# Three joints of a three-block network kernel: the last square goes into the means by matmul, a table load is issued ahead, first matmuls wait for less, and branch outputs are rounded in two steps

## The reference, cut to what matters

```python
def rms_norm(x, g):
    xf = x.astype(jnp.float32)
    y = xf * lax.rsqrt(jnp.mean(xf * xf, axis=-1, keepdims=True) + EPS)
    return (y * g.astype(jnp.float32)).astype(x.dtype)
...
# first block, end of the mixer
y = gates[:, :, 0] * y_a + gates[:, :, 1] * y_b + gates[:, :, 2] * y_c
return y @ lp['w_out'], s_f, s_b
...
# first block
h_lat = h_lat + g1 * yl
h_lat = h_lat + g2 * swiglu(modulate(rms_norm(h_lat, norm2_g[l]), sh2, sc2), w_ffn_in[l], w_ffn_out[l])
...
# second block ends in a feed-forward layer and a norm; the third begins with a norm and a projection
return _rmsnorm(x, final_norm)
...
h = rms_norm_3(x, norm_g) * (1.0 + scale[:, None, :]) + shift[:, None, :]
z = h @ w_in
```

## Time and profile before

| | us |
|---|---|
| median of 3 runs | 3472.44 |
| lowest and highest | 3472.02, 3476.12 |
| the profiled execution | 3478.79 |
| its span in the trace | 3477.0 |
| TensorE busy in it | 3398.7 (98%) |

### The profile page before, as it was taken

The page is one execution under the profiler, slowest core; times in us unless marked ns, Lnnn a source line. Parts: engine busy times, 40 slices in busy tenths (PEclk is TensorE's granted clock), DMA queues, the critical chain, the costliest instruction groups (busy, mean ns, idle before and its releaser), DMA issues.

```text
span 3477.0 us, 38568 instructions
## 1 busy us (share of the span) xinstructions
PE 3398.7 (98%) x15758; PEld 2725.9 (78%) x15758; DVE 1234.8 (36%) x2140; ACT 1249.2 (36%) x1988; POOL 1475.5 (42%) x674
## 2 busy tenths in 40 slices
PE   8999999998999999999999999999999999999998
PEld 5777788887888888887677888888887778888776
DVE  3266775623221134212553111211123642111554
ACT  4534323533222232223554222322233653222543
POOL 4322445654544444445424444444436234444332
PEclk9999999999999999999999999999999999999999
DMA  7211233442333323434213333333333123333211
GB/s 272 67 55 61 97 97 121 157 140 73 122 127 128 98 96 135 139 97 117 67 34 103 97 96 94 94 99 97 94 104 101 39 76 97 97 95 99 73 61 55
DMA packets 102174, 345.41 MB, mean 99 GB/s; under 512 B 12173, under 2 KB 12557, under 8 KB 101838
## 3 DMA queue, kind: packets, MB, share of 16 engines
q1 hardware_dynamic: 101200, 341.10, 30.9%
q10 hardware_dynamic: 798, 1.85, 0.2%
HBM read 336.08 MB, written 2.10 MB: 97 GB/s over the span
## 4 chain that ended last, share of the span: by engine, by line
PE 89%; DVE 4%; ACT 2%; DMA 2%; POOL 1%; issue 1%; SPq 0%; ACTq 0%; DVEq 0%
PE ps L1201 25%; PE ps L1203 24%; PE ps L1202 24%; PE ps L1232 2%; PE ps L1233 2%; PE ps L1234 2%; PE ps L1502 2%; PE ps L1532 1%; DMA t<-in_w_ada 1%; PE ps L1515 1%; POOL t L2675 1%; DVE t L2105 1%; PE ps L1421 1%; PE ps L1435 0%; ACT t L1893 0%
## 5 line engine op out<-in xcount | busy, mean ns | idle before, releaser
L2675 POOL TENSOR_TENSOR t<-t,t 128x1024 fp32r<-128x1024 f32 (+2 forms) x584 | 1354.4, 2321 | 1886.4 <-ACT t L1590 1882.4
L1201 PE MATMUL ps<-t,t 128*128 128x512 f32 x4016 | 1597.8, 398 | 19.6 <-POOL t L2675 13.7
L1203 PE MATMUL ps<-t,t 128*128 128x512 f32 x4016 | 1573.1, 392 | 0.0
L1202 PE MATMUL ps<-t,t 128*128 128x512 f32 x4016 | 1568.4, 391 | 0.0
L1201 PEld LDWEIGHTS ps<-t,t 128*128 128x128 f32 x4016 | 758.0, 189 | 196.0 <-issue 24.1
L1203 PEld LDWEIGHTS ps<-t,t 128*128 128x128 f32 x4016 | 757.4, 189 | 166.1
L1202 PEld LDWEIGHTS ps<-t,t 128*128 128x128 f32 x4016 | 758.3, 189 | 157.7 <-issue 1.7
L1590 ACT CAST t<-t 128x1024 fp32r<-128x1024 f32 (+2 forms) x588 | 584.1, 995 | 575.1 <-PE ps L1203 414.9
L2454 DVE TENSOR_TENSOR t<-t,ps 128x512 f32<-128x512 f32 x110 | 75.7, 688 | 537.0 <-PE ps L1203 522.4
L1656 ACT CAST t<-t 128x512 fp32r<-128x512 f32 x158 | 97.2, 622 | 408.0 <-DVE t L2454 357.5
L1849 ACT ACTIVATE t<-t 128x512 f32<-128x512 f32 x88 | 55.6, 632 | 311.7 <-DVE t L2447 311.6
(11 more groups left out here) (296 smaller groups left out, 2225.3 us busy)
## 6 DMA issues: line engine op xcount, KB each, us to landing
t<-in_w_f1i SPq DMA_DIRECT2D x88, 512.0 KB, 3.6
t<-in_w_f2i SPq DMA_DIRECT2D x88, 512.0 KB, 3.6
t<-in_w_ada SPq DMA_DIRECT2D x72, 512.0 KB, 4.5
t<-in_w_ffi SPq DMA_DIRECT2D x44, 512.0 KB, 4.1
t<-in_w_f1o SPq DMA_DIRECT2D x32, 512.0 KB, 3.5
t<-in_w_f2o SPq DMA_DIRECT2D x32, 512.0 KB, 3.5
t<-in_w_gate SPq DMA_DIRECT2D x24, 512.0 KB, 4.3
t<-in_w_out SPq DMA_DIRECT2D x48, 256.0 KB, 2.7
```

Of the source, the lines that this page charges most:

```text
L1201: e.matmul(out, wh[:, at], X.hi[c][:, 0:N], start=c == first, stop=False)
L1202: e.matmul(out, wh[:, at], X.lo[c][:, 0:N], start=False, stop=False)
L1203: m = e.matmul(out, wl[:, at], X.hi[c][:, 0:N], start=False, stop=c == final)
L2675: e.tensor_tensor(k.WL[:, n % NHL, 0:w], k.raw[:, j % NRAW, 0:w], f(k.WH[:, n % NHL, 0:w]), ALU.subtract).then_inc(*k.rest.inc(('rest', j) ...
```

## The change

Four edits. (1) A sum may be `split`: the last square isn't added by VectorE; the sum of the first seven goes through four mean matmuls as before, and the last square goes through four more that accumulate in the same bank. The sums `n2` and `n3` are split. (2) At such a joint ScalarE computes one unused square root (`root_table`) after tile 6's squares, so that the table with the root is loaded there. (3) In `products`, the first matmul of a channel tile waits only for the hi part if the input is `y`, `n2` or `n3`, and the second waits for lo. (4) `mixture` splits `y` in steps: tiles 0 to 2 after output tile 5, tiles 3 to 6 after output tile 6, tile 7 last; lo of tiles 0 and 2 is on GpSimd, all others on VectorE. A 32-byte tile, `k.spare`, is added ahead of `k.mask`.

```diff
@@ -134,7 +134,7 @@
 class Sum:
 
     last = 7
-    bank = False
+    bank = split = False
 
     def __init__(self, tag, acc, n=S, prior=None, vector=(), first=None, since=()):
         self.tag, self.acc, self.n, self.prior, self.vector, self.first, self.since = (tag, acc, n, prior, vector, first, since)
@@ -145,8 +145,8 @@
         return ring(k, 'sq ' + self.tag, k.tmp[self.first:], self.since)
 
 
-def banked(sq):
-    sq.bank = True
+def banked(sq, split=False):
+    sq.bank, sq.split = (True, split)
     return sq
 
 
@@ -199,6 +199,7 @@
     k.ada = sbuf(k, [128, 64])
     k.ada3 = sbuf(k, [128, 24])
     k.sm = sbuf(k, [128, 128])
+    k.spare = sbuf(k, [128, 1])
     k.mask = sbuf(k, [128, 2, 128], BF16)
     k.tmp = [sbuf(k, [128, S]) for _ in range(4)]
     k.cols = Slots([sbuf(k, [128, 8]) for _ in range(4)])
@@ -564,12 +565,10 @@
     YA = k.XA('y')
 
     def mixture(i):
-        for j in range(i + 1 if i == 6 else 0):
+        for j in {5: (0, 1, 2), 6: (3, 4, 5, 6), 7: (7,)}[i]:
             on.mixture(YA, j)
-        if i == 7:
-            on.mixture(YA, 7)
     branch(on, 1, 'oconv', XA, k.CN, lambda j: ada() if j < 5 else None, done=mixture)
-    res = Residual('out1', lambda j: k.ada[:, 16 + j:17 + j], banked(Sum('n2', k.R[0], S, ('center', 7))), [('ada', 'ada', 2)])
+    res = Residual('out1', lambda j: k.ada[:, 16 + j:17 + j], banked(Sum('n2', k.R[0], S, ('center', 7)), split=True), [('ada', 'ada', 2)])
     for n in range(KT):
         if n == 0:
             on.T2((('out1', 0), 'out', 0), (('out1', 1), 'out', 1), YA)
@@ -621,7 +620,7 @@
             on.T((wo, i - LEAD), wo, i - LEAD, B)
             beside(i)
             on.gated(g, wo, i - LEAD)
-        if i >= KT and done is not None:
+        if i >= KT - 1 and done is not None:
             done(i - LEAD)
 
 
@@ -842,7 +841,7 @@
     scale = res.sum
     nxt = banked(Sum('fin2' if layer else 'f1_1', k.R[1 - layer], S, ('fox', L, 7), range(8) if layer else (), 2, [('lo', ('mid', 'f2_' + L), FF - 1)]))
     if layer:
-        twin = banked(Sum('n3', k.R[2], S, None, range(8)))
+        twin = banked(Sum('n3', k.R[2], S, None, range(8)), split=True)
         twin.slots = nxt.slots
         res = Residual('f2_1', lambda j: 0.5, nxt, scale=scale, twin=twin, by=lambda j: k.sm[:, 24 + j:25 + j])
         on.twin_gain('final2', 1)
@@ -1197,8 +1196,12 @@
         self.wait_ge('rest', i)
         for c in ks:
             at = slice(128 * (c - c0), 128 * (c - c0) + 128)
+            if X.tag in ('n2', 'n3', 'y'):
+                self.wait_ge('hi', X.tag, c)
+            else:
+                self.wait_ge('lo', X.tag, c)
+            e.matmul(out, wh[:, at], X.hi[c][:, 0:N], start=c == first, stop=False)
             self.wait_ge('lo', X.tag, c)
-            e.matmul(out, wh[:, at], X.hi[c][:, 0:N], start=c == first, stop=False)
             e.matmul(out, wh[:, at], X.lo[c][:, 0:N], start=False, stop=False)
             m = e.matmul(out, wl[:, at], X.hi[c][:, 0:N], start=False, stop=c == final)
         return m
@@ -1264,16 +1267,23 @@
         k, e = (self.k, self.e)
         b = self.take(k.banks, 'means', sq.tag)
         self.wait_ge('load', 'con')
-        self.wait_ge('ssq', sq.tag, sq.last)
+        self.wait_ge('ssq', sq.tag, sq.last - sq.split)
         for t in range(sq.n // 128):
-            m = e.matmul(b[:, 2 * t:2 * t + 2], sq.acc[:, t * 128:t * 128 + 128], const(k, 'mean')[:, 0:2], start=True, stop=True)
-        m.then_inc(*k.filled.inc(('filled', ('means', sq.tag))))
+            m = e.matmul(b[:, 2 * t:2 * t + 2], sq.acc[:, t * 128:t * 128 + 128], const(k, 'mean')[:, 0:2], start=not sq.split or t == 0, stop=not sq.split, skip_group_check=True)
+        if not sq.split:
+            m.then_inc(*k.filled.inc(('filled', ('means', sq.tag))))
+            return
+        self.wait_ge('sq', sq.tag, sq.last)
+        own = sq.slots(k).of(('sq', sq.tag, sq.last))
+        for t in range(sq.n // 128):
+            m = e.matmul(b[:, 2 * t:2 * t + 2], own[:, t * 128:t * 128 + 128], const(k, 'mean')[:, 0:2], start=False, stop=True, skip_group_check=True)
+        m.then_inc(*k.filled.inc(('filled', ('means', sq.tag)), ('ssq', sq.tag, sq.last), ('free', ('sq', sq.tag, sq.last))))
 
     def square(self, sq, t, src, ready):
 
         if sq.bank and t == 0:
             self.take(self.k.banks, 'sum', sq.tag, hold=True)
-        if sq.bank and t == sq.last:
+        if sq.bank and t == sq.last - sq.split:
             self.k.banks.let(('sum', sq.tag))
 
     def residual(self, res, n, key, since=None):
@@ -1836,6 +1846,13 @@
                 self.settle()
             self.square(res.twin, n, self.k.X[:, n, :], ('x', res.tag, n), res.by(n))
         self.square(res.sum, n, self.k.X[:, n, :], ('x', res.tag, n))
+        if n == 6 and (res.sum.split or (res.twin is not None and res.twin.split)):
+            self.root_table()
+
+    def root_table(self):
+
+        k, e = (self.k, self.e)
+        e.activation(k.spare, const(k, 'one')[:, 0:1], ACT.Sqrt).then_inc(*k.act.inc())
 
     def ffn_gate(self, m, i):
         k, e = (self.k, self.e)
@@ -2054,8 +2071,10 @@
 
     def square(self, sq, t, src, ready):
         k, e = (self.k, self.e)
+        if sq.split and t == sq.last:
+            return
         if t and sq.bank:
-            b, end = (self.bank('sum', sq.tag)[:, 0:sq.n], t == sq.last)
+            b, end = (self.bank('sum', sq.tag)[:, 0:sq.n], t == sq.last - sq.split)
             self.wait_ge('sq', sq.tag, t)
             self.wait_ge('ssq', sq.tag, t - 1)
             if end and sq.prior:
@@ -2393,7 +2412,7 @@
             self.low(k.CN, i, k.CA[:, i, :], *([('normed', 'cn', 7)] if i == 7 else []))
 
     def mixture(self, A, j):
-        if j % 2:
+        if j not in (0, 2):
             self.low(A, j, self.k.O[:, j, :])
 
     def scale_parts(self, event, A, n, g, since):
@@ -2721,7 +2740,7 @@
             e.tensor_tensor(k.CA[:, i, :], k.CA[:, i, :], k.R[0], ALU.subtract).then_inc(*k.pool.inc(('center', i)))
 
     def mixture(self, A, j):
-        if j % 2 == 0:
+        if j in (0, 2):
             self.low(A, j, self.k.O[:, j, :])
 
     def residual(self, res, n, key, since=None):
```

## The result

The changed kernel takes 3484.78 us in the median of 7 runs (3480.85 to 3486.29), against 3472.44 of the kernel before on the same chip (7 runs). The ratio is 1.0029 (95% interval 1.002 to 1.0039), so it is slower, by 10 us (7 to 13.5). That ratio is taken over all the runs; the two medians alone lie 12.3 us apart. Forecast was 3464.5 and faster. The time came out on the side of the rival *Slower*.

The account below looks back on a forecast made before the run. TensorE, busy 98% of the span, was taken as the bound, so only its waits and lower clock cost time. Terms of 6.3 + 0.8 + 0.8 = 7.9 us off 3472.44 gave 3464.5 us, range 3462.5 to 3468.5.

Parts of the forecast that it names:

- Slower: Five down projections: k.spare moves tiles to odd multiples of 32 bytes, read slower; 3482.6 us at 3%, chance 0.04.
- The last of the prediction's own signs of being wrong: Away from the joints: the prediction is wrong if matmul spacing there isn't 0.228 us.
- The sum of the change, 7.9 us: Whole kernel: 6.3 us at the first joint plus 0.8 us at each of the two norm joints.
- First joint, 6.3 us: Before the pair of 'out1': two-step rounding shortens TensorE's gap by 3.3 us to 2.2, plus 3.0 us of clock.
- the 3.0 us of clock: Behind the first joint's gap: the clock stays at 1.00, so 15 slow matmuls no longer cost 3.0 us more.
- Contention on GpSimd: First joint: VectorE beside GpSimd slows lo parts, 1.37 us against 0.69 alone on VectorE, but hidden; uncontended sum 9.2 us.
- Second joint, 0.8 us: Norm before the feed-forward pair: the last means start when ScalarE's square is done, about 843.55 instead of 844.36.
- Third joint, 0.8 us: Norm after the twin sums: the last square by matmul lets the means start at 3220.25 instead of 3221.08.
- Table ahead, hi waits, 0 each: Norm joints: early table load gains 0 itself but lets the 0.8 us stand; waiting for hi alone gains 0, at most 0.4.

Follow-up runs that it names:

- h2_d480_0: The change with k.spare last, 32 unused bytes ahead of WH and 448 ahead of k.mask, run once: 3505.26 us.
- e1_spare_last: The changed kernel with only the 32-byte spare tile moved to the end of SBUF, all four edits kept: 3464.80 us, ratio 0.9981 to the kernel before.
- g1_branch_only: The kernel before with only the two-step branch rounding: 3466.87 us, ratio 0.9988 to the kernel before.
- g2_norms_only: The change at its old addresses without the two-step branch rounding: 3471.40 us, ratio 0.9999 to the kernel before.
- f1_change_448: The change with k.spare last and 448 unused bytes ahead of k.mask: 3457.48 us, ratio 0.9963 to the kernel before.
- f2: The kernel before with 64 unused bytes ahead of the weight tiles WH and WL, moving all behind them too: 3521.87 us in one run.
- h3: The change with k.spare last, 128 unused bytes ahead of WH and 256 ahead of k.mask, run once: 3506.39 us.
- h4: The change with k.spare last, 448 unused bytes ahead of WH and 224 ahead of k.mask, run once: 3502.74 us.
- e2_shift32: The kernel before with 32 unused bytes ahead of k.mask and no edit: 3493.57 us, ratio 1.0059 to the kernel before.
- e4_shift64: The kernel before with 64 unused bytes ahead of k.mask and no edit: 3493.94 us, ratio 1.0057 to the kernel before.
- i1_before_448: The kernel before with 448 unused bytes ahead of k.mask and no edit: 3468.90 us, ratio 0.9989 to the kernel before.

## Why the prediction was wrong

**The step that failed is the rival's, "No row shows a large operand at such an address; nothing speaks for it", and its chance of 0.04.** The spare tile was in the diff, its effect on all addresses behind it was seen, its price was worked out per matmul (a turn at 3.0 ns each), and then it got next to nothing. It cost 4.4 ns each in the down projections, 1.9% of 0.2289 us, and 15.7 us in all spacings, against 7.9 us forecast to be won; 4.0 of the 15.7 fell in stages with arena tiles that the rival hadn't counted. The last of the prediction's own signs of being wrong, a spacing other than 0.228 us away from the joints, is the one that came. And something did speak for it. The prediction took 0.228 us as the one spacing at full clock, but the trace of before has two, 0.2267 and 0.2289, for the same instruction with the same shapes. Its two windows above show it: 451 in 100 us (435 products and 16 narrow ones, so 0.2267 each with 0.09 for a narrow one) against 438. Such a difference between equal instructions points at what does differ, the operands. Had I asked which tiles were the moving ones, I would have found HH and HL against the arena, and the rival would have had a size and a good chance. The rival's mechanism itself was wrong: not the odd multiple of 32 (the down projections of `h2_d480_0` stand there and are at their fastest), but the distance. That its 3482.6 us lies near the measured time is therefore luck as well.

**The sum of the change, 7.9 us, stands** as far as measured: `e1_spare_last` won 6.6 (3.5 to 9.7). By its terms:

- *First joint, 6.3 us.* From the last branch output on VectorE to the first residual of 'out1', 7.1 us were won in the changed kernel, and 76 matmuls across the joint take 6.8 us less in `g1_branch_only`. TensorE resumes 1.34 us after the stop rather than 2.2, and the clock held, as chosen. In all ten traces with the edit no matmul behind this gap is slow. One thing in the term was too large: the 3.0 us of clock. The profile of before had the longest recovery of the six traces without the edit, which show 7 to 14 slow matmuls (14 in that of before, 10.7 on average). Against `g2_norms_only`, with 7, the 76 matmuls take 24.59 us, so the edit wins 5.5 to 7 us by the traces, within the interval of `g1_branch_only`.
- *Contention on GpSimd.* The two lo parts took 2.55 us for the 2.8 taken, the rests 2.37 to 2.41. Where VectorE worked beside it, in `g2_norms_only`, four lo parts took 1.64 us each. The 1.37 us that the prediction read for a lo part of VectorE is a mean of one at 0.68, begun while GpSimd stood idle, and two at 1.79 beside it; and VectorE took over two lo parts, those of tiles 4 and 6, not four. Both were hidden, so the sum doesn't change. The Trainium skill (GPSIMD Engine Reference, Specifications) has the two engines contend, and the traces agree.
- *Second joint, 0.8 us.* The means that count start 1.47 us after the last residual (836.41) in place of 2.29: 0.8 won. Then the row products take 2.05 us, as the clock fell to 0.65 in that window, against 1.57 before. 0.3 us is left: VectorE's first scaling comes 5.21 us after the last residual in place of 5.52. The forecast did not ask where in the norm the clock falls. In `f1_change_448` it held there, and the row products are short (timeline, then windows):

```profile
833.62 1.05 PE L1280 MATMUL ps<-t,t 128*128 128x2 f32 x8 [0.72 <-ACT t L1634]
835.27 1.18 PE L1301 MATMUL ps<-t,t 128*128 128x128 f32 x8 [0.59 <-DVE t L2139]
838.11 0.76 PE L1204 MATMUL ps<-t,t 128*128 128x512 f32 x1 [1.66 <-ACT t L1660]
...
834.00:836.00 2.00, 1.41 (x13) 1.00 0.73 258
```

From means to the next product it is 4.49 us there, 5.36 in the changed kernel, 5.63 before (where that product also waits for lo). That part of the gain depends on where the clock falls, and with the same norm edits it fell at different places.
- *Third joint, 0.8 us.* The means start 2.29 us after the last residual in place of 3.11, 0.8 won, but they take 1.86 us for 1.02, and all of it is given back. This and the 0.3 us above are readings of one execution. From the 20th product ahead of the norm to the 100th behind it, six traces with the norm edits take 35.77 to 37.23 us at the second joint and 39.59 to 42.91 at the third, six without them 36.83 to 38.41 and 41.20 to 43.74 (without `f2`, `h2`, `h3` and `h4`, whose products with HH and HL are slower). The means are 1.0 and 0.8 us lower with the edits, near the forecast but inside the scatter, and at the second joint the two-step rounding has a part in it: among the traces that have it, the means are 36.5 with the norm edits and 36.8 without.
- *Table ahead, hi waits, 0 each.* The table is loaded at 3210.73, and no load stands between the last square (3225.49) and the root (3227.54); the first product at 843.24 is released by ScalarE's hi part. Nothing else shows either. The Trainium skill (ScalarE: Activation LUTs, What ACT_TABLE_LOAD costs) would have the preload win 1.6 us more at the second joint; the means started 0.8 us sooner and the root with them, so no drain was there to be won. In the changed kernel the load at 832.41 takes 1.28 us and the unused root starts right behind it, at 833.70.

**Against the total:** 15.7 lost in spacing less 6.6 won is 9.1; measured 10 (7 to 13.5).

**What stays open.** Why a distance costs what it does. In the down projections the spacing repeats in threes, 229, 232, 226 ns before and 237, 231, 232 after; no run here looks into the reason. A distance of 160 wasn't tried, nor one that is no multiple of 32. Kernels without the branch edit that had only addresses moved came out slower than their spacing says (`e2_shift32` 20 us for 15.7, `e4_shift64` 20 for 14.0, `i1_before_448` won 3.8 for 9.3), each with a median granted clock 0.001 to 0.003 below before. Why the clock answers so isn't settled.

## What to carry to other kernels

A tile of 32 bytes cost more here than four scheduling edits won: after any change of the allocation, compare the spacing of matmuls at full clock, stage by stage, and put new small tiles behind all large ones. Where the same matmul has two spacings in one trace, look at the distance between its moving and its weight tile modulo 256 bytes first; making it 0 was worth about as much here as the best edit. And when the time gained lies in an idle stretch of TensorE, ask in which instruction the clock will fall, since a chain that starts 0.8 us sooner can still end at its old time.

## What the runs showed of the hardware

- The spacing of these 128x512 matmuls with four-byte (fp32r) operands went by the distance between the moving and the weight tile in a partition, modulo 256 bytes as far as tried: 0.2267 us at 0, 0.2289 at 64, 0.2324 to 0.2333 at 32, 96, 128, 192 and 224, at a granted clock of 1.00.
- The own alignment of the tiles made no difference where it was tried: 0.2267 us at odd multiples of 32 bytes in `h2_d480_0`.
- Behind a gap of one length the lower clock lasted for 7 to 14 matmuls in six executions with a gap of 5.75 to 5.94 us from start to start.
- GpSimd's 128x512 subtraction took 1.26 to 1.30 us alone and 1.73 to 1.77 beside a subtraction of VectorE, VectorE's took 0.68 to 0.69 when it began with GpSimd idle and 1.73 to 1.80 beside GpSimd (`before`, `after`, `g2_norms_only`, first joint).
